# Two neighbouring weight slots filled by one transfer, in a fused block of two attention mixers

## The chip, the cores and the metric

The kernel runs on one core of one Trainium2 chip. The metric is the device time of one launch in microseconds; the median of three runs stands for a kernel. One more execution is profiled, and its trace gives the rows below. Engines are named as the profile names them: PE is TensorE (PEld its weight loads), DVE VectorE, ACT ScalarE, POOL GpSimd, SP SyncE, which here only issues transfers.

## What is computed

One layer on 256 tokens of width 2048, in float32: a normalisation, one input projection to 9296 columns, two groups of eight attention heads, gating, an output projection, the residual and a last normalisation.

```python
h = rms_norm(x, norm_gain[l])
proj = jnp.einsum('btd,de->bte', h, w_in[l])
qa, ka, va, ga, qb, kb, vb, gb, qi, ki, wi = jnp.split(proj, offsets, axis=-1)
out_a = chunked_relpos_attention(heads(qa, H_A), heads(ka, H_A), heads(va, H_A), rel_bias[l])
out_b = dsa_sparse_attention(heads(qb, H_B), heads(kb, H_B), heads(vb, H_B), qi, ki, wi, slopes)
ya = out_a.reshape(B, T, D_A) * jax.nn.silu(ga)
yb = out_b.reshape(B, T, D_B) * jax.nn.silu(gb)
x = x + jnp.einsum('bte,ed->btd', jnp.concatenate([ya, yb], axis=-1), w_out[l])
return rms_norm(x, final_gain)
```

Mixer A is softmax attention with a learned bias by relative position; with 256 tokens its band covers all earlier chunks of 64. Mixer B picks the 64 best keys of each query by an indexer (`qi`, `ki`, `wi`) and attends to these with a distance penalty.

## The kernel before

**Blocks and units.** The weights of both projections are read once, as 22 blocks of 512 columns (numbers 0 to 21). Blocks 0 and 1 make values (1 with the narrow index columns beside), 2 and 3 the indexer's queries, 4 to 7 queries and keys of mixer B, 8 and 9 the remaining values, 10 to 13 queries and keys of mixer A, 14 to 17 the gates, 18 to 21 the output projection. A block has 8 units; a unit is 256 rows by 512 columns of weights, 512 KB, laid out as 128 partitions of 4 KB.

**The ring.** A unit passes through a ring of RING = 4 slots. SyncE loads it into `w_raw[:, u % 4]` and counts on `w_landed[u % 4]`. ScalarE's `split_hi` (L752 to L759) rounds it to float32r into `hi_slots`; it waits for the landing and for `mm_done`, TensorE's count of finished units, because TensorE must have read the slot four units back. VectorE's `split_lo` (L1076 to L1081) subtracts and writes what is left to `lo_slots`, and counts `lo_done`. TensorE's `unit` (L520 to L529) waits for `lo_done` and runs 12 matmuls of 512 columns: two row blocks, two token tiles, three products (hi by hi, hi by lo, lo by hi). Since `split_lo` is the last reader of the raw slot, SyncE may load a unit as soon as `lo_done` counts the unit four back.

**The order on the engines** is written out by hand. Each engine runs its own list in order and waits on semaphores. In the pair blocks (10 to 17) each block g carries, between the splits, the attention of one head pair, pair = g - 10. On ScalarE (`pair_attention`, L973): exponentials, split of unit 6, `planes_out` (L951: the probabilities' 32-bit words are taken apart into two planes of 16 bits), split of unit 7, the splits of units 0 and 1 of the next block, staging of the next pair's queries and keys, `pT_out` (L956: wait for the turned planes, put the words together again, L958, round, L960), split of unit 2, `projection_out` of the block just finished, splits of units 3 to 5. VectorE has the same splits in its list, with `pT_rest` (L1429) after those of units 0 and 1. TensorE runs `score_pair` after unit 1 of block g and `value_pair` (L692), which waits for `pT_rest`, after unit 0 of block g + 1. There is one value_pair per pair; that of pair 7 stands after unit 2 of block 18.

**Turns.** Activations that are needed with tokens and features exchanged are turned by transposing transfers on 16-bit planes. SyncE issues them, in between the loads, from the same queue: `turn_planes(pair)` (L385) after the load of unit 2 of block g + 1, and `turn_projection(n)` (L410) after the load of unit 6. n = 0 to 3 are queries and keys of mixer B, 4 to 7 those of mixer A, 8 to 11 the gates; the planes of n are made by VectorE (n < 4) or GpSimd, and put together by ScalarE or GpSimd. The last of them, n = 11, is issued in block 18; its product, the last gates, goes through ScalarE's `tanh_gates` and VectorE's `gated`, then `y_hi` and `y_lo` (L1469, with `ylo_done`), and TensorE waits for `y_lo(6)` before unit 6 of block 18. A turn waits for its planes first (`planes_made`, `proj_split`), and while it waits, the loads behind it wait as well.

**The loads that the change touches** are those of blocks 4 to 17 (`token_block`, L401) and 18 to 21 (`out_unit`, L426, the last three blocks in a hardware loop): 144 loads, each behind a wait on `lo_done`.

Of the kernel before, what the change touches and what calls it, by code (L numbers as in the profile page):

```python
# [43 lines left out]
G_TOKENS = 4  # L44
G_WIDE, G_QI, G_INDEX, G_VB, G_VA, G_QKA, G_GATE, G_OUT, G_END = 1, 2, 3, 8, 9, 10, 14, 18, 22
ROW_VB, VA_FIRST, ROW_VA = 6, 8, 9
UK = 2
UNITS = KT // UK
RING = 4
# [9 lines left out]
def hybrid_block(nc, xT, x, norm_gain, w_blocks, w_narrow, rel_bias, wo_blocks, final_gain, out):  # L59
# [6 lines left out]
    ds = bass.ds  # L66

    with ExitStack() as ctx:
        def sb(name, shape, dt=f32):
            return ctx.enter_context(nc.sbuf_tensor(name, shape, dt))  # L70
# [4 lines left out]
        def sem(name):  # L75
            return ctx.enter_context(nc.semaphore(name))
# [5 lines left out]
        w_raw = raw_slots[:, :, 0:UK * CB]  # L82
# [13 lines left out]
        o = sb("o", [P, 4, TM, CB])  # L96
# [56 lines left out]
        w_landed = [sem(f"w_landed{s}") for s in range(RING)]  # L153
        hi_done = sem("hi_done")
        lo_done = sem("lo_done")
# [130 lines left out]
        rows = (slice(0, IDX_D), slice(IDX_D, P))  # L286
# [35 lines left out]
        def narrow_loads(p):  # L322

            return sum(kind == BROAD and q % RING == p % RING for q, (kind, _) in enumerate(STARTS[:p + 1]))
# [15 lines left out]
        def _(sp):  # L340
            def load(u, src):
                sp.dma_start(w_raw[:, u % RING, :], src).then_inc(w_landed[u % RING], 16)


            def load_features(u, rows):
                half, j = u // 4, u % 4
                c = (j % 2) * CB + half * T
                sp.dma_start(w_raw[:, u % RING, :].rearrange("p (q c) -> p q c", q=4),
                             rows[:, 4 * (j // 2):4 * (j // 2) + 4, c:c + T]).then_inc(w_landed[u % RING], 16)
# [10 lines left out]
            for u in range(HALVED):  # L360
                for kk in range(UK):
                    c = slice(kk * CB, kk * CB + CB)
# [22 lines left out]
            def turn_planes(pair):  # L385
                sp.wait_ge(planes_made, pair + 1)
                sp.dma_start_transpose(flat(planes_T).rearrange("p (t q) -> p t q", q=P),
                                       flat(planes)).then_inc(planes_turned, 16)
# [10 lines left out]
                        turn_small(*turns)  # L399

            def token_block(g, row, pair=None, n=None):  # L401
                for u in range(UNITS):
                    sp.wait_ge(lo_done, g * UNITS + (u - RING + 1))
                    load(u, w_blocks[ds(row, 1), u, :, :].rearrange("o p c -> (o p) c"))
                    if u == 2 and pair is not None:
                        turn_planes(pair)
                    if u == 6 and n is not None:
                        turn_projection(n)

            def turn_projection(n):  # L410
                sp.wait_ge(proj_split, n + 1)
                source, turned = proj_planes(n)
                sp.dma_start_transpose(flat(turned).rearrange("p (t q) -> p t q", q=P),
                                       flat(source)).then_inc(proj_turned, 16)
# [3 lines left out]
            for g in range(G_TOKENS, G_VA):  # L418
                token_block(g, g - G_QI if g < G_VB else ROW_VB + 1, n=g - G_TOKENS - 1 if g > G_TOKENS else None)
            token_block(G_VA, ROW_VA)  # L420
            token_block(G_QKA, G_QKA)
            for pair in range(HEADS - 1):
                g = pair + G_QKA + 1
                token_block(g, g, pair, pair + N_LATE)

            def out_unit(g, u):  # L426
                sp.wait_ge(lo_done, g * UNITS + (u - RING + 1))
                load(u, wo_blocks[ds(g - G_OUT, 1), u, :, :].rearrange("o p c -> (o p) c"))

            for u in range(UNITS):  # L430
                out_unit(G_OUT, u)
                if u == 2:
                    turn_planes(HEADS - 1)
                if u == 6:
                    turn_projection(N_END - 1)
            with sp.Fori(G_OUT + 1, G_END) as g:
                for u in range(UNITS):
                    out_unit(g, u)

            for n, (m, c) in enumerate(VECTOR_PARTS):  # L440
                sp.wait_ge(vector_scaled, n + 1)
# [309 lines left out]
        def _(act):  # L751
            def split_hi(g, c):  # L752

                u = c % UNITS
                s = u % RING
                act.wait_ge(w_landed[s], g * (16 * UNITS // RING) + 16 * (c // RING + 1))
                if not (isinstance(g, int) and g * UNITS + c < RING):
                    act.wait_ge(mm_done, g * UNITS + (c - RING + 1))
                nc.scalar.activation(hi_slots[:, s, 0:UK * CB], w_raw[:, s, :], ACT.Copy).then_inc(hi_done, 1)  # L759
# [55 lines left out]
            for p, (kind, u) in enumerate(STARTS):  # L815
                if p >= 2 * HALVED:
                    if kind == PLAIN:
                        act.wait_ge(xT_landed[u], 16)
                        for k in range(UK * u, UK * u + UK):
                            a_part(k)  # L820
                        split_hi(0, p)
                    else:
                        split_hi_wide(p)
                    for v in SQUARES.get(p, ()):
                        square_x(v)
                if p == len(STARTS) - 2:
                    nc.scalar.preload_act_table(ACT.Sqrt)
# [7 lines left out]
            for c in range(4):  # L835
                split_hi(G_QI, c)
# [4 lines left out]
            for c in range(4, 8):  # L841
                split_hi(G_QI, c)
                if c == 6:
                    features_low(G_QI, 0, QT)
# [165 lines left out]
            g = G_OUT - 1  # L1010
# [570 lines left out]
```

## Time and profile before

| | us |
|---|---|
| median of three runs | 516.11 (516.06 to 516.22) |
| the profiled execution | 516.02 |
| its span, first to last instruction | 514.2 |
| TensorE busy | 505.7 |
| VectorE busy | 354.3 |
| ScalarE busy | 305.7 |
| GpSimd busy | 70.1 |
| weight transfers (mean of all 16 transfer engines, over the span) | 67.4% of their time |

The difference between the profiled execution's time and its span lies ahead of the first and behind the last instruction of the program. Busy time is an average over the whole span; what a wait costs is read from the stretch in which it happens. A matmul's end is modelled, so successive matmuls overlap in the trace: what counts is the distance of their starts.

### The profile page before, as it was taken

To read this page: it belongs to the slowest core of one execution; us is meant where nothing else is said; L and a number is where in the kernel's file an instruction comes from. 1 tells how busy PE (TensorE), PEld (TensorE's weight loads), DVE (VectorE), ACT (ScalarE), POOL (GpSimd) and SP (SyncE) were. 2 spreads that over 40 slices of the span, in tenths; PEclk is the share of its full clock that TensorE was granted. 3 is DMA by queue.
4 is the path that set the end of the run, shared out by engine and by line. 5 is a ranking of instruction groups with operands and counts; after the bars stand their busy time and mean duration, and the time that the engine had idled before them with its cause. 6 is when DMAs were issued, how large, how long until landed. Compare 5 with 4: busy or idle time off the path is not lost.

```text
span 514.2 us, 6764 instructions
## 1 busy us (share of the span) xinstructions
PE 505.7 (98%) x2476; PEld 430.1 (84%) x2476; DVE 354.3 (69%) x517; ACT 305.7 (59%) x410; POOL 70.1 (14%) x61
## 2 busy tenths in 40 slices
PE   8999999999999999999999999999999999999994
PEld 6989999888888888888888888888888888888883
DVE  5897777765856686876777766666768687746554
ACT  6866555446564555445866758584959586545342
POOL 1000053150500000000111130303021313000000
PEclk9999999999999999999999999999999999999998
DMA  8974898658685876563768676877677779775614
GB/s 270 401 234 142 215 296 265 241 184 237 236 256 164 246 208 224 201 193 102 246 198 240 212 245 215 214 216 205 194 206 229 233 222 267 266 223 178 202 41 164
DMA packets 77358, 112.23 MB, mean 218 GB/s; under 512 B 44144, under 2 KB 53264, under 8 KB 77200
## 3 DMA queue, kind: packets, MB, share of 16 engines
q1 hardware_dynamic: 75472, 106.38, 67.4%
q0 software_dynamic: 1568, 5.01, 3.0%
q10 hardware_dynamic: 288, 0.46, 0.3%
q8 instruction: 17, 0.28, 0.2%
q14 instruction: 13, 0.11, 0.1%
HBM read 99.24 MB, written 2.11 MB: 197 GB/s over the span
## 4 chain that ended last, share of the span: by engine, by line
PE 98%; DMA 1%; DVE 0%; ACT 0%; issue 0%; DVEq 0%; POOLq 0%
PE acc L516 26%; PE acc L518 25%; PE acc L517 25%; PE acc L547 5%; PE acc L567 4%; PE acc L575 3%; PE acc L551 2%; PE aux L577 2%; DMA gain<-norm_gain 1%; PE aux L688 1%; PE aux L698 1%; PE aux L686 0%; PE aux L703 0%; PE aux L704 0%; PE aux L685 0%; PE aux L705 0%
## 5 line engine op out<-in xcount | busy, mean ns | idle before, releaser
L1080 DVE TENSOR_TENSOR lo_slots<-raw_slots,hi_slots 128x1024 fp32r<-128x1024 f32 x166 | 210.4, 1278 | 108.7 <-ACT hi_slots L759 108.1
L759 ACT ACTIVATE hi_slots<-raw_slots 128x1024 fp32r<-128x1024 f32 x166 | 174.0, 1056 | 127.4 <-PE acc L518 110.0
L516 PE MATMUL acc<-hi_slots,acts 128*128 128x512 f32 x576 | 225.4, 391 | 0.0
L518 PE MATMUL acc<-hi_slots,acts 128*128 128x512 f32 x576 | 224.2, 389 | 0.0
L517 PE MATMUL acc<-lo_slots,acts 128*128 128x512 f32 x576 | 224.2, 389 | 0.0
L518 PEld LDWEIGHTS acc<-hi_slots,acts 128*128 128x128 f32 x576 | 108.1, 188 | 22.8
L516 PEld LDWEIGHTS acc<-hi_slots,acts 128*128 128x128 f32 x576 | 108.2, 188 | 22.1 <-DVE acts L1471 0.3
L517 PEld LDWEIGHTS acc<-lo_slots,acts 128*128 128x128 f32 x576 | 108.2, 188 | 21.8
L547 PE MATMUL acc<-acts,hi_slots 128*128 128x384 f32 x128 | 34.3, 349 | 0.0
L491 POOL COPY o<-z 128x2048 uint16<-128x2048 uint16 x4 | 7.6, 1899 | 159.7 <-ACT z L874 159.7
L551 PEld LDWEIGHTS acc<-acts,lo_slots 128*128 128x128 f32 x128 | 23.1, 188 | 0.0
L551 PE MATMUL acc<-acts,lo_slots 128*128 128x192 f32 x128 | 23.1, 262 | 0.0
L547 PEld LDWEIGHTS acc<-acts,hi_slots 128*128 128x128 f32 x128 | 19.4, 191 | 0.0
L944 ACT ACTIVATE probs<-probs,neg_top,q_rate 128x256 f32<-128x256 f32 (+1 forms) x16 | 8.6, 536 | 17.4 <-DVE neg_top L1392 17.4
L567 PE MATMUL acc<-hi_slots,acts 128*128 128x512 f32 x64 | 17.9, 394 | 0.3 <-DVE acts L1109 0.3
L575 PE MATMUL acc<-hi_slots,acts 128*128 128x320 f32 x64 | 18.0, 308 | 0.0
L577 PE MATMUL aux<-hi_slots,acts 128*128 128x272 f32 x64 | 17.6, 286 | 0.0
L958 ACT ACTIVATE probs_T<-qiT 128x1536 uint16<-128x1536 uint16 x8 | 15.6, 1947 | 2.3 <-DMA qiT<-qiT 2.3
L491 POOL COPY v<-z 128x2048 uint16<-128x2048 uint16 x4 | 8.0, 2010 | 53.7 <-ACT z L874 53.7
L497 POOL COPY z<-t_gate 128x2048 uint16<-128x2048 uint16 x4 | 12.1, 3024 | 21.4 <-DMA t_gate<-v 21.4
L567 PEld LDWEIGHTS acc<-hi_slots,acts 128*128 128x128 f32 x64 | 11.5, 188 | 3.9 <-DVE acts L1109 1.7
L947 ACT ACTIVATE probs<-probs,neg_max 128x256 f32<-128x256 f32 (+1 forms) x16 | 7.1, 446 | 11.8 <-DVE neg_max L1388 11.8
(172 smaller groups left out, 481.5 us busy)
## 6 DMA issues: line engine op xcount, KB each, us to landing
raw_slots<-w_blocks SPq DMA_DIRECT2D x140, 512.0 KB, 4.3
raw_slots<-wo_blocks SPq DMA_DIRECT2D x32, 512.0 KB, 4.2
raw_slots<-w_blocks SPq DMA_DIRECT2D x8, 256.0 KB, 5.2
qk<-xT SPq DMA_DIRECT2D x7, 256.0 KB, 5.3
qk<-x POOLq DMA_DIRECT2D x1, 1536.0 KB, 8.1
o<-ext_dram POOLq DMA_DIRECT2D x1, 1024.0 KB, 7.3
fgain<-final_gain POOLq DMA_DIRECT2D x1, 1024.0 KB, 4.8
out<-o SPq DMA_DIRECT2D x2, 512.0 KB, 3.0
```

Source lines behind the costliest of these rows:

```text
L491: nc.gpsimd.tensor_copy(proj_planes(n)[0], halves(z)).then_inc(proj_split, 1)
L516: nc.tensor.matmul(dst, a_hi[:, k, t], hi, start=start, stop=False)
L517: nc.tensor.matmul(dst, a_hi[:, k, t], lo, start=False, stop=False)
L518: return nc.tensor.matmul(dst, a_lo[:, k, t], hi, start=False, stop=stop)
L547: nc.tensor.matmul(whole, w_hi4[:, u % RING, q, f * HD:f * HD + HD], acts[:, k, :, tokens], start=(k == 0), stop=False)
L551: last = nc.tensor.matmul(acc[:, bank:bank + n], w_lo4[:, u % RING, q, f * HD:f * HD + HD], a_hi[:, k, tokens], start=False, stop=(k == KT ...
L567: last = nc.tensor.matmul(acc[:, m * CB:m * CB + CB], a[:, k, m * P:m * P + P], w[:, p % RING, c], start=start, stop=stop)
L575: nc.tensor.matmul(acc[:, (TM + m) * CB:(TM + m) * CB + PART], a[:, k, t], w[:, p % RING, c:c + PART], start=start, stop=stop)
L577: last = nc.tensor.matmul(aux[m][:, 0:REST], a[:, k, t], w[:, p % RING, c + PART:c + WIDE], start=start, stop=stop)
L759: nc.scalar.activation(hi_slots[:, s, 0:UK * CB], w_raw[:, s, :], ACT.Copy).then_inc(hi_done, 1)
L958: nc.scalar.activation(halves(probs_T), planes_T, ACT.Copy).then_inc(words_made, 1)
L1080: nc.vector.tensor_tensor(lo_slots[:, s, 0:UK * CB], w_raw[:, s, :], hi_slots[:, s, 0:UK * CB].bitcast(f32), ALU.subtract).then_inc(lo_don ...
```

## The change

From block 4 on, SyncE loads two units with one transfer of 1 MB into slots 0 and 1 or slots 2 and 3. The transfer waits for what its second unit's load waited for, and counts on the semaphore of the first slot alone; ScalarE waits on that semaphore for both units. So 144 transfers become 72. The turns keep their place behind the transfer that has unit 2, or unit 6; that transfer has unit 3, or unit 7, in it now. Nothing changes on VectorE, TensorE and GpSimd.

```diff
             def load(u, src):
                 sp.dma_start(w_raw[:, u % RING, :], src).then_inc(w_landed[u % RING], 16)
 
+            def load_two(g, u, rows):
+                sp.wait_ge(lo_done, g * UNITS + (u + 1 - RING + 1))
+                sp.dma_start(w_raw[:, u % RING:u % RING + 2, :],
+                             rows[:, u:u + 2, :, :].rearrange("o u p c -> p (o u) c")).then_inc(w_landed[u % RING], 16)
+
...
             def token_block(g, row, pair=None, n=None):
-                for u in range(UNITS):
-                    sp.wait_ge(lo_done, g * UNITS + (u - RING + 1))
-                    load(u, w_blocks[ds(row, 1), u, :, :].rearrange("o p c -> (o p) c"))
+                for u in range(0, UNITS, 2):
+                    load_two(g, u, w_blocks[ds(row, 1), :, :, :])
                     if u == 2 and pair is not None:
                         turn_planes(pair)
                     if u == 6 and n is not None:
...
-            def out_unit(g, u):
-                sp.wait_ge(lo_done, g * UNITS + (u - RING + 1))
-                load(u, wo_blocks[ds(g - G_OUT, 1), u, :, :].rearrange("o p c -> (o p) c"))
-
-            for u in range(UNITS):
-                out_unit(G_OUT, u)
+            def out_units(g, u):
+                load_two(g, u, wo_blocks[ds(g - G_OUT, 1), :, :, :])
+
+            for u in range(0, UNITS, 2):
+                out_units(G_OUT, u)
                 if u == 2:
                     turn_planes(HEADS - 1)
                 if u == 6:
                     turn_projection(N_END - 1)
             with sp.Fori(G_OUT + 1, G_END) as g:
-                for u in range(UNITS):
-                    out_unit(g, u)
+                for u in range(0, UNITS, 2):
+                    out_units(g, u)
...
                 s = u % RING
-                act.wait_ge(w_landed[s], g * (16 * UNITS // RING) + 16 * (c // RING + 1))
+                together = not isinstance(g, int) or g * UNITS + c >= G_TOKENS * UNITS
+                act.wait_ge(w_landed[s - s % 2 if together else s], g * (16 * UNITS // RING) + 16 * (c // RING + 1))
```

## Rows read from the trace of the kernel before

**Rows 1.** The page: busy time, and the chain that ended last

```profile
PE 505.7 (98%) x2476; PEld 430.1 (84%) x2476; DVE 354.3 (69%) x517; ACT 305.7 (59%) x410; POOL 70.1 (14%) x61
PE 98%; DMA 1%; DVE 0%; ACT 0%; issue 0%; DVEq 0%; POOLq 0%
```

**Rows 2.** By stretch: us; PE, PEld, DVE, ACT, POOL busy; PEclk; DMA; GB/s

```profile
79.00:507.00 428.00, 428.00 (x2007) 358.96 (x2005) 290.87 (x416) 253.63 (x338) 60.09 (x37) 1.00 0.69 211
507.00:514.00 7.00, 0.02 (x1) 0.00 (x0) 2.76 (x6) 1.84 (x4) 0.00 (x0) 0.76 0.54 202
```

**Rows 3.** Groups by line: busy, mean ns, idle before and its releasers

```profile
L759 ACT ACTIVATE hi_slots<-raw_slots 128x1024 fp32r<-128x1024 f32 x166 | 174.0, 1056 | 127.4 <-PE acc L518 110.0 <-PE acc L551 7.1 <-DMA raw_slots<-w_blocks 4.0
```

**Rows 4.** Timeline of SyncE's queue, pair 0: start us, duration, instruction

```profile
243.01 0.33 SPq L342 DMA_DIRECT2D raw_slots<-w_blocks  x1
243.39 1.54 SPq L387 DMA_TRANSPOSE qiT<-qiT  x1
245.60 0.48 SPq L342 DMA_DIRECT2D raw_slots<-w_blocks  x1
```

**Rows 5.** Timeline of SyncE's queue: pair 4's turn, the last projection turn

```profile
337.36 2.27 SPq L387 DMA_TRANSPOSE qiT<-qiT  x1
422.40 2.60 SPq L413 DMA_TRANSPOSE t_gate<-v  x1
```

**Rows 6.** Timeline, pairs 0, 1, 3, 4, 7: copy, low part, value_pair

```profile
251.00 0.69 DVE L1432 TENSOR_TENSOR parts_lo<-probs_T,parts_hi 128x512 fp32r<-128x512 f32 x1 [2.22 <-ACT parts_hi L960]
252.07 0.38 PE L698 MATMUL aux<-probs_T,v 128*128 128x128 f32 x2
274.43 0.69 DVE L1432 TENSOR_TENSOR parts_lo<-probs_T,parts_hi 128x512 fp32r<-128x512 f32 x1 [1.82 <-ACT parts_hi L960]
276.22 0.38 PE L698 MATMUL aux<-probs_T,v 128*128 128x128 f32 x2
321.89 0.69 DVE L1432 TENSOR_TENSOR parts_lo<-probs_T,parts_hi 128x512 fp32r<-128x512 f32 x1 [1.89 <-ACT parts_hi L960]
324.53 0.38 PE L698 MATMUL aux<-probs_T,v 128*128 128x128 f32 x2
342.88 1.94 ACT L958 ACTIVATE probs_T<-qiT 128x1536 uint16<-128x1536 uint16 x1
345.51 0.69 DVE L1432 TENSOR_TENSOR parts_lo<-probs_T,parts_hi 128x512 fp32r<-128x512 f32 x1 [1.48 <-ACT parts_hi L960]
348.68 0.49 PE L698 MATMUL aux<-probs_T,v 128*128 128x128 f32 x3
419.83 1.97 ACT L958 ACTIVATE probs_T<-qiT 128x1536 uint16<-128x1536 uint16 x1
```

**Rows 7.** Timeline of the first output block: VectorE and TensorE

```profile
423.45 1.23 DVE L1080 TENSOR_TENSOR lo_slots<-raw_slots,hi_slots 128x1024 fp32r<-128x1024 f32 x1 [0.26 <-ACT hi_slots L759]
435.27 0.68 DVE L1471 TENSOR_TENSOR acts<-o,acts 128x512 fp32r<-128x512 f32 x1
435.47 0.39 PE L517 MATMUL acc<-lo_slots,acts 128*128 128x512 f32 x1
435.70 0.39 PE L518 MATMUL acc<-hi_slots,acts 128*128 128x512 f32 x1
436.01 0.50 PE L516 MATMUL acc<-hi_slots,acts 128*128 128x512 f32 x1
```

**Rows 8.** Stretches as rows 2; landing of L387's, L413's turns; loads issued

```profile
149.00:151.50 2.50, 2.50 (x13) 2.07 (x12) 0.17 (x1) 2.30 (x3) 0.00 (x0) 1.00 1.02 419
243.90:245.90 2.00, 2.00 (x10) 1.68 (x9) 1.55 (x2) 2.00 (x3) 0.00 (x0) 1.00 0.79 239
DMA to landing us min/median/max: 4.8/4.9/5.0
DMA to landing us min/median/max: 4.3/4.4/6.6
raw_slots<-w_blocks SPq DMA_DIRECT2D x140, 512.0 KB, 4.3
```

## Prediction

> **What bounds the kernel now.** I read the page's engine line and chain of waits first [rows 1]: TensorE is busy for 98% of the span, and the chain that ended last is TensorE for 98%. Then the busy time by stretches [rows 2]: from 79 to 507 us, the whole stretch that the change touches, TensorE is busy for 428 of 428 us; only the last 7 us are not matmul. Two things follow. No part of the weight stream is on the path today: no load can make the time shorter by landing earlier, since no matmul waits for one. And any wait that is new for TensorE is paid in full, because there is no idle time of TensorE later that could take it back. So the question is only whether something that TensorE needs becomes later than TensorE. The waits say how the stream runs [rows 3]: ScalarE's high-part splits wait 110 us for TensorE to give their slot back, and for a load of w_blocks only twice, 4.0 us. The loads have room. I then looked, row by row, at what else SyncE issues: the transposing transfers ("turns").
>
> **Fewer, larger loads.** 144 loads of 512 KB become 72 of 1 MB. The even unit of each pair now leaves with the odd one, one unit later (a unit is 12 matmuls that start 0.23 us apart [rows 7], 2.7 us), and lands with the whole megabyte. Price of the second half in the transfer engines: in a stretch with loads queued one behind the other they move 419 GB/s, so 1.25 us [rows 8]; while a lone load starts up, 239 GB/s, so 2.2 us. The even unit is thus 4 to 5 us later at its slot. I price that at nothing: ScalarE waits for TensorE and not for the load [rows 3], and behind its split stand the other slots of the ring, split and not yet multiplied. That ring of four is the cover; if it were gone, each late load would cost its lateness in full. SyncE's saved issues (0.33 us each [rows 4]) are off the path: worth 0.
>
> **The turn of the probabilities, eight times.** For each head pair SyncE issues the turn (L387) after the load of unit 2. In pair 0 the load leaves at 243.01, the turn 0.38 later at 243.39, as soon as ScalarE has made the planes, and the load of unit 3 at 245.60 [rows 4]. The load of unit 3 is the interesting row: it goes as soon as the low-part split of unit 7 of the block before is done. In the changed kernel units 2 and 3 are one transfer that waits for just that split, and the turn stands behind it. So the turn leaves at 245.60 + 0.38 = 245.98, 2.6 us later. The same distance of some 2.2 us stands between turn and next load in the other pairs, since the split of unit 7 follows the planes on ScalarE, and its low part that on VectorE, in a fixed order.
> On top comes the queue. A turn takes 4.8 to 5.0 us from issue to landing with 512 KB issued 0.38 us ahead of it; the projection turns, whose load went out 1.8 us earlier, take as little as 4.3 [rows 8]. So a turn waits behind the load in front of it, and a load of twice the size should cost it the second half: between 0 and 2.2 us. I take 1.25, the rate of queued loads, because the second half follows on a stream that is already running. Delay of the landing: 2.6 + 1.25 = 3.85 us (2.6 to 4.8).
>
> Who waits for it: ScalarE copies the turned planes (L958, L960), VectorE splits off the low part (L1432), then TensorE's value_pair (L698) starts, after unit 0 of the next block. Queued behind the copy on ScalarE are the high-part splits of the next units; they have more room than value_pair. How much room: the end of L1432 against the start of L698 [rows 6]. Pair 0: 251.69 and 252.07, 0.38 us. Pair 1: 275.12 and 276.22, 1.1. Pair 3: 322.58 and 324.53, 1.95; pair 2 lies between, near 1.7. Pair 4: 346.20 and 348.68, 2.48, and there ScalarE was busy with its list until 342.88 while the turn landed at most 5.0 after its issue at 337.36 [rows 5, 8], so 0.5 more: 3.0. Pairs 5 and 6 repeat pair 4. In pair 7 ScalarE reaches its copy at 419.83, 4.5 us later than three further blocks of 24.15 (324.53 to 348.68) would put it: no cost. When TensorE does wait it loses a little more: at 436.01 it starts 0.06 after VectorE's row ends and that matmul takes 0.50 instead of 0.39 [rows 7], so I take 0.17 off each room.
> Since the score of the next pair is a TensorE step behind value_pair, each wait moves the next pair's chain along with TensorE; the next pair has its old room and pays again. Pair 0: 3.85 - 0.2 = 3.65. Pair 1: 2.9. Pair 2: 2.3. Pair 3: 2.05. Pairs 4 to 6: 3.85 - 2.8 = 1.05 each, 3.1. Sum 14.0 us.
>
> **The turn of the gate projection, at the end.** The projection turns (L413) stand behind unit 6's load and will stand behind units 6 and 7. Of twelve, the first four also wait for VectorE's plane copy, which comes after the split that gates the new load, and what the next seven bring is read a block or more later: 0, the cover being that block. The last one has no block behind it. It leaves at 422.40 [rows 5], and GpSimd joins the words, which VectorE's and ScalarE's gating wait for, down to the low part of the gated activations (L1471, ends 435.95), on which TensorE's row at 436.01 already waits [rows 7]. The new transfer of units 6 and 7 waits for the low-part split that begins at 423.45 and ends at 424.68 [rows 7]; the turn leaves 0.4 later, at 425.07: 2.67 us late. It also falls from 1.8 us behind 512 KB to 0.38 behind 1 MB. Bounds for that: 0, and the second half plus the lost distance, 2.2 + 1.4. I take 2.2: the megabyte lands 1.25 after the 4.3 us that a half takes [rows 8], 5.2 after the turn's own issue, and the turn some 1.5 us after that, 6.7 where it now takes about 4.5. Sum 4.9 us.
>
> **Sum.** The profiled execution took 516.02 us (span 514.2, the rest around it), 0.1 below the median of the three runs. 516.0 + 14.0 + 4.9 = 534.9; on the median's scale **535.0 us**. With the queue's price at 0: 2.4 + 1.7 + 1.1 + 0.8 + 2.7 = 8.7, 524.8. With the half at 239 GB/s: eight more places with 0.95 each, 542.5.
>
> **Rivals.**
> *The queue costs the turns nothing.* Only the 2.6 us of later issue remain: 524.8 as above. For it: the turn's transfer might be prepared while the load still runs. Against: a turn right behind a load already takes 0.6 longer than one with distance [rows 8]. It is also where we would land if VectorE and ScalarE won back, during TensorE's first wait, what later pairs lack. Chance 0.14.
> *The queue costs more*, the half at start-up rate: 542.5. For it: the load in front of a turn is always the first after a pause. Chance 0.1.
> *TensorE's clock falls during the waits.* The granted clock is 1.00 (2.4 GHz) through the whole busy stretch and 0.76 on average over the last 7 us, where TensorE has nothing to do: there it fell to the lower level [rows 2]. The two longest waits, 3.65 at pair 0 and 4.9 at the end, are the candidates. At 1.2 GHz the 0.23 us of a matmul double, so one unit at the low level costs 2.7 us more: two such, 540.3. The Trainium skill says so too ("TensorE: Matmul & The Clock Gate", Part 1): the throttled state is the default and activity releases it, so idling has a price after the idling. The trace agrees as far as its last row goes; no wait inside the busy stretch shows it. Chance 0.2.
> *Not slower.* With half as many transfers to issue and complete, the turn passes the queue faster than now and lands when it is needed. It decides at 0.2 us of delay in pair 0 and 0 at the end. To get there a turn would have to win 2.4 us of 4.9, and the best projection turn, with its load well ahead, took 4.3 [rows 8]. A gain beyond that isn't there to be had, as TensorE has no wait to lose. Time 516.0. Chance 0.05, of which 0.01 is a run that comes out faster.
> *A load becomes late*, in the stretches where ScalarE already reaches its split as the load lands: more than 543. By my estimate a megabyte would have to take twice what I price. Chance 0.04.
>
> **How the numbers follow.** The forecast as summed has 0.47. The range takes the queue's two bounds, 524.7 to 542.5; the clock's case lies in it. What is left out is the not slower case, the late load and part of the tails. A measurement here tells about 0.2% (1 us) from no change; all cases but one are far over it: slower 0.95, same 0.04, faster 0.01.
>
> **What would show it.** In the trace of after: waits of TensorE at L698 for VectorE L1432, largest in the first pair and shrinking to about 1 us in pairs 4 to 6, none in pair 7; one wait of about 5 us before unit 6 of block 18 for L1471; turns that leave 0.4 behind their load and land 6 us or more after issue; ScalarE's L958 waiting for the turn in pairs 0 to 6. If TensorE waits at L516 for L1080 instead, it is the loads. If the turns land 5 us after issue, the queue's price was wrong; if the waits at L698 don't come back pair after pair, the assumption that the chain moves along with TensorE was. If L698 doesn't wait at all, the step on the room is wrong.

## The result: 559.9 us, and the profile after

The changed kernel takes 559.86 us (median of four runs, 557.09 to 564.97) against 516.16 us before: 1.086 times as long (95% interval 1.082 to 1.090). Forecast were 535.0 us and a range of 524.7 to 542.5. The direction came as predicted, and so did the way in which the late turns of the probabilities stop TensorE; most of what is missing comes from two terms that the sum has at nothing. The profiled execution of after took 561.64 us, 1.8 above the median; its span is 559.8 us, 45.6 more than before, and the readings below are made against that span.

The page of after: busy time, the chain that ended last, and three groups by line (busy, mean ns, idle before and releaser).

```profile
PE 520.7 (93%) x2476; PEld 440.1 (79%) x2476; DVE 362.3 (65%) x517; ACT 305.3 (55%) x410; POOL 66.7 (12%) x61
PE 23%; DMA 11%; ACT 9%; DVE 9%; issue 4%; SPq 1%; POOL 0%; DVEq 0%; ACTq 0%; POOLq 0%
L701 PE MATMUL aux<-probs_T,v 128*128 128x128 f32 x32 | 7.1, 356 | 23.6 <-DVE parts_lo L1436 23.6
L519 PE MATMUL acc<-hi_slots,acts 128*128 128x512 f32 x576 | 229.4, 398 | 7.0 <-DVE acts L1475 7.0
L962 ACT ACTIVATE probs_T<-qiT 128x1536 uint16<-128x1536 uint16 x8 | 15.4, 1921 | 32.7 <-DMA qiT<-qiT 32.7
```

The lines have moved by 3 to 5 (value_pair L698 is L701, `split_lo` L1080 is L1084, the copy L958 is L962, the low part L1432 is L1436, the turns L387 and L413 are L392 and L417, GpSimd's join L497 is L500). In place of 98% TensorE [rows 1], the chain now runs through the turns (DMA), their copies on ScalarE and the low parts on VectorE. TensorE waits 23.6 us at value_pair, in seven pairs, and 7.0 us once, before unit 6 of block 18. And it is busy for 15.0 us more with the same 2476 matmuls. This says why, by stretches (columns as in [rows 2]): seven stretches of the busy part in which the granted clock is 0.50, the lower of the two levels (1.2 GHz).

```profile
255.02:261.85 6.83, 4.26 (x15) 3.88 (x16) 4.07 (x4) 5.56 (x7) 1.89 (x1) 0.50 0.16 67
316.46:319.87 3.41, 3.41 (x11) 2.74 (x11) 2.54 (x3) 2.13 (x3) 1.89 (x1) 0.50 0.00 0
343.77:350.60 6.83, 5.88 (x19) 5.11 (x20) 5.17 (x4) 4.16 (x6) 1.89 (x1) 0.50 0.09 10
374.49:377.90 3.41, 3.41 (x14) 3.12 (x15) 2.47 (x2) 3.08 (x5) 1.89 (x1) 0.50 0.02 5
405.21:408.62 3.41, 3.41 (x10) 2.62 (x9) 2.54 (x3) 1.79 (x2) 1.89 (x1) 0.50 0.00 0
432.51:435.92 3.41, 3.41 (x13) 2.97 (x12) 2.54 (x2) 2.68 (x4) 1.89 (x1) 0.50 0.00 0
476.89:483.72 6.83, 3.96 (x9) 3.14 (x10) 6.72 (x8) 5.17 (x6) 0.00 (x0) 0.50 0.74 271
sum 34.13, PE 27.74 PEld 23.58 DVE 26.05 ACT 24.57 POOL 11.36; mean PE 3.96 PEld 3.37 DVE 3.72 ACT 3.51 POOL 1.62
```

Two matmuls of 512 columns in the second of these stretches, from TensorE's timeline:

```profile
317.20 0.63 PE L520 MATMUL acc<-lo_slots,acts 128*128 128x512 f32 x1
317.63 0.63 PE L521 MATMUL acc<-hi_slots,acts 128*128 128x512 f32 x1
```

TensorE worked for 27.74 us in the seven stretches. Such matmuls start 0.427 us apart there, elsewhere 0.227, so by this spacing 27.74 x (1 - 0.227/0.427) = 13.0 us of the time is the clock. The whole difference then reads: 24.8 us of waits at value_pair (from the end of the matmul before, by starts), 7.2 at the end, 0.4 early (at 128.6 us, where ScalarE's copy waits 1.9 us for the first projection turn, which landed 7.6 us after its issue in place of 4.6), 13.0 of clock. Sum 45.4 of 45.6.

The timeline of pair 0 and of the end, SyncE's queue, ScalarE, VectorE and TensorE:

```profile
245.84 0.37 SPq L346 DMA_DIRECT2D raw_slots<-w_blocks  x1
246.25 1.97 SPq L392 DMA_TRANSPOSE qiT<-qiT  x1
254.24 1.91 ACT L962 ACTIVATE probs_T<-qiT 128x1536 uint16<-128x1536 uint16 x1 [6.65 <-DMA qiT<-qiT]
256.84 0.69 DVE L1436 TENSOR_TENSOR parts_lo<-probs_T,parts_hi 128x512 fp32r<-128x512 f32 x1 [7.82 <-ACT parts_hi L964]
257.59 1.22 PE L701 MATMUL aux<-probs_T,v 128*128 128x128 f32 x4 [5.13 <-DVE parts_lo L1436]
...
457.18 1.06 ACT L763 ACTIVATE hi_slots<-raw_slots 128x1024 fp32r<-128x1024 f32 x1 [3.17 <-DMA raw_slots<-wo_blocks]
464.14 0.37 SPq L346 DMA_DIRECT2D raw_slots<-wo_blocks  x1
464.55 5.14 SPq L417 DMA_TRANSPOSE t_gate<-v  x1
471.82 2.46 POOL L500 COPY z<-t_gate 128x2048 uint16<-128x2048 uint16 x1 [10.47 <-DMA t_gate<-v]
479.76 0.80 PE L519 MATMUL acc<-hi_slots,acts 128*128 128x512 f32 x1 [7.01 <-DVE acts L1475]
```

Here the predicted chain is to be seen link by link: the load, the turn 0.41 behind it at 246.25 (before 243.39 [rows 4]; ScalarE's planes are only 0.2 us later than in the kernel before), ScalarE waiting for the landing, VectorE, TensorE. What was not predicted is how late it lands: 7.96 us after its issue.

Landing of the turns in after, the planes' (L392) and the projections' (L417); before it was 4.9 and 4.4 in the median [rows 8]:

```profile
DMA to landing us min/median/max: 6.4/6.6/8.7
DMA to landing us min/median/max: 5.6/7.1/9.2
```

### The profile page after: what moved, and what is told of

Its sections match the earlier page's. It is cut to its first block, busy times and chain, and to the rows that moved or that the text cites. A ratio compares the mean times of both kernels' runs of the same rounds, so it can differ in the third digit from the quotient of the medians.

```text
span 559.8 us, 6656 instructions
## 1 busy us (share of the span) xinstructions
PE 520.7 (93%) x2476; PEld 440.1 (79%) x2476; DVE 362.3 (65%) x517; ACT 305.3 (55%) x410; POOL 66.7 (12%) x61
## 4 chain that ended last, share of the span: by engine, by line
PE 23%; DMA 11%; ACT 9%; DVE 9%; issue 4%; SPq 1%; POOL 0%; DVEq 0%; ACTq 0%; POOLq 0%
DMA qiT<-qiT 8%; PE acc L519 7%; PE acc L520 7%; PE acc L521 7%; DVE lo_slots L1084 3%; ACT hi_slots L763 3%; ACT probs_T L962 3%; DVE probs L1430 2%; DMA raw_slots<-wo_blocks 1%; DMA t_gate<-v 1%; ACT probs L948 1%; PE aux L701 1%; ACT probs L951 1%; DVE parts_lo L1436 1%; DVE probs L1407 1%
## 5 line engine op out<-in xcount | busy, mean ns | idle before, releaser
L1084 DVE TENSOR_TENSOR lo_slots<-raw_slots,hi_slots 128x1024 fp32r<-128x1024 f32 x166 | 211.4, 1285 | 111.9 <-ACT hi_slots L763 111.3
L519 PE MATMUL acc<-hi_slots,acts 128*128 128x512 f32 x576 | 229.4, 398 | 7.0 <-DVE acts L1475 7.0
L520 PE MATMUL acc<-lo_slots,acts 128*128 128x512 f32 x576 | 227.9, 396 | 0.0
L521 PE MATMUL acc<-hi_slots,acts 128*128 128x512 f32 x576 | 227.3, 395 | 0.0
L519 PEld LDWEIGHTS acc<-hi_slots,acts 128*128 128x128 f32 x576 | 110.9, 193 | 30.1 <-DVE acts L1475 7.4
L521 PEld LDWEIGHTS acc<-hi_slots,acts 128*128 128x128 f32 x576 | 110.4, 192 | 23.6
L520 PEld LDWEIGHTS acc<-lo_slots,acts 128*128 128x128 f32 x576 | 110.5, 192 | 22.4
L962 ACT ACTIVATE probs_T<-qiT 128x1536 uint16<-128x1536 uint16 x8 | 15.4, 1921 | 32.7 <-DMA qiT<-qiT 32.7
L1436 DVE TENSOR_TENSOR parts_lo<-probs_T,parts_hi 128x512 fp32r<-128x512 f32 x8 | 5.5, 692 | 41.5 <-ACT parts_hi L964 41.5
L701 PE MATMUL aux<-probs_T,v 128*128 128x128 f32 x32 | 7.1, 356 | 23.6 <-DVE parts_lo L1436 23.6
L701 PEld LDWEIGHTS aux<-probs_T,v 128*128 128x128 f32 x32 | 5.4, 235 | 26.7 <-DVE parts_lo L1436 26.6
L550 PEld LDWEIGHTS acc<-acts,hi_slots 128*128 128x128 f32 x128 | 19.4, 191 | 0.0
L570 PE MATMUL acc<-hi_slots,acts 128*128 128x512 f32 x64 | 18.1, 397 | 0.0
L958 ACT ACTIVATE qiT<-probs 128x1536 uint16<-128x1536 uint16 x8 | 11.9, 1485 | 11.3 <-DVE probs L1430 11.3
```

What stands on the lines that cost most here:

```text
L519: nc.tensor.matmul(dst, a_hi[:, k, t], hi, start=start, stop=False)
L520: nc.tensor.matmul(dst, a_hi[:, k, t], lo, start=False, stop=False)
L521: return nc.tensor.matmul(dst, a_lo[:, k, t], hi, start=False, stop=stop)
L550: nc.tensor.matmul(whole, w_hi4[:, u % RING, q, f * HD:f * HD + HD], acts[:, k, :, tokens], start=(k == 0), stop=False)
L570: last = nc.tensor.matmul(acc[:, m * CB:m * CB + CB], a[:, k, m * P:m * P + P], w[:, p % RING, c], start=start, stop=stop)
L701: nc.tensor.matmul(aux[3][:, h * T + P:h * T + T], v1_flat[:, c], pT1[:, h, :], start=(h == 0), stop=False, skip_group_check=True)
```

## The experiments

The main theory: the turns stand one unit later and behind a whole megabyte, and what hangs on them stops TensorE; the clock falls on top. Rivals: the larger transfer itself is slow or starves the ring; the planes' turns alone do it; or the clock is the larger half and the waits the smaller.

### Each turn ahead of the transfer

After, with each turn issued before the load that it stood behind (in the first output block alike):

```diff
                 for u in range(0, UNITS, 2):
-                    load_two(g, u, w_blocks[ds(row, 1), :, :, :])
                     if u == 2 and pair is not None:
                         turn_planes(pair)
                     if u == 6 and n is not None:
                         turn_projection(n)
+                    load_two(g, u, w_blocks[ds(row, 1), :, :, :])
...
```

> The 72 transfers of 1 MB stay, but each turn is issued ahead of the transfer of units 2 and 3 (or 6 and 7) and not behind it. If the late turns are the whole loss (A), TensorE has no wait for VectorE's L1432 or L1471 split rows again and the time is that of before, 516 us, within 2 us. If the megabyte loads come too late for the splits (B; ScalarE's idle time for loads grew from 6.4 to 23.5 us in the changed kernel), the waits for loads stay and the time stays over 530 us.

Measured: 523.80 us, 1.014 of before (1.0125 to 1.0159), between the two expected cases. So 36 of the 44 us are the turns' place behind the loads, with all that follows from it. No wait at value_pair is left, and the planes' turns land in 3.7 us, faster than in the kernel before; the landing of L392 and of the projection turns (L417), and three waits (total, times, longest):

```profile
DMA to landing us min/median/max: 3.6/3.7/3.7
DMA to landing us min/median/max: 4.3/4.3/4.9
...
ACT hi_slots L763 <- DMA raw_slots<-w_blocks: 52.7, 26, 6.8
PE aux L627 <- ACT t_gate L864: 3.6, 2, 1.9
PE acc L519 <- DVE lo_slots L1084: 1.5, 1, 1.5
```

The 3.7 us is what the prediction lacked: the price of a planes' turn with nothing in front of it. The 7.6 us that stay are paid elsewhere. ScalarE waits 52.7 us for loads (4.0 before [rows 3]), since a turn that waits for its planes now holds up the load of two units; in blocks 5 and 6 the split that ScalarE is late with stands ahead of a copy (L864) that TensorE's L627 needs, 1.9 us at most, with 3.4 us at the lower clock behind the second wait; and once, in block 19, a low part is late, behind a load that landed 9.9 us after its issue while GpSimd's 1.5 MB transfer of x ran.

### The old transfers, the turns one unit later

Before, with the planes' turns behind unit 3's load and the projections' behind unit 7's; the loads stay 512 KB:

```diff
-                    if u == 2 and pair is not None:
+                    if u == 3 and pair is not None:
                         turn_planes(pair)
-                    if u == 6 and n is not None:
+                    if u == 7 and n is not None:
                         turn_projection(n)
...
```

> The kernel before, with its 144 loads of 512 KB, and only the turns moved: the turn of the probabilities behind the load of unit 3, the projection's behind that of unit 7. The turn leaves 2.6 us later as in the changed kernel, but with two loads of 512 KB ahead of it, one of them 2.6 us older. (A) order and transfer size share the loss: turns land about 5 us after issue instead of 6.5, waits of about 2.4, 1.7, 1.1 and 0.8 us in pairs 0 to 3, 3 us at the end: 525 to 530 us. (B) the loads alone: 516 us. (C) the order alone is the loss, the queue costs nothing: as the changed kernel, 555 to 562 us.

Measured: 540.10 us, 1.045 (1.0427 to 1.0480), more than expected. The wait at value_pair (total, times, longest), the landing of the turns (L387), and VectorE and GpSimd in pair 4:

```profile
PE aux L698 <- DVE parts_lo L1432: 14.1, 7, 3.5
...
DMA to landing us min/median/max: 4.8/4.9/7.1
...
347.80 3.26 DVE L1426 TENSOR_SCALAR probs<-probs,p_inv 128x256 f32<-128x256 f32 x4
...
348.01 2.52 POOL L497 COPY qk<-o 128x2048 uint16<-128x2048 uint16 x1 [7.35 <-DMA o<-o]
```

The later issue was as expected, 2.6 us in every pair, and the turns landed after 4.8 to 4.9 us in pairs 1 to 6 (6.4 in pair 0). But by starts the waits at value_pair were 3.69, 2.65, 1.65, 1.63, 1.88, 1.85 and 1.90, where they should have fallen to next to nothing by pair 4 by the rooms of [rows 6]; 3.1 us stood at the end, and 10.2 us passed at the lower clock. In pairs 3 to 6 the four normalising rows of VectorE (L1426), 1.01 us in all in the kernel before, took 2.1 to 3.3 us: GpSimd's join of a projection turn had moved onto them. In pairs 1 and 2 it stood on a row ahead of them (L1392, 2.52 and 2.09 us in place of 0.23). That was the first sight of a term that the prediction has at nothing.

### Old transfers in pairs

Before, with two 512 KB loads issued back to back where the megabyte would go, the turns behind both:

```diff
-                for u in range(UNITS):
-                    sp.wait_ge(lo_done, g * UNITS + (u - RING + 1))
-                    load(u, w_blocks[ds(row, 1), u, :, :].rearrange("o p c -> (o p) c"))
+                for u in range(0, UNITS, 2):
+                    sp.wait_ge(lo_done, g * UNITS + (u + 1 - RING + 1))
+                    for v in (u, u + 1):
+                        load(v, w_blocks[ds(row, 1), v, :, :].rearrange("o p c -> (o p) c"))
...
```

> The changed kernel's order and gates, but each 1 MB transfer issued as two of 512 KB, one right after the other on the same queue, 144 transfers again. (A) what delays a turn is the bytes that stand ahead of it: turns land 6.4 us after issue as behind the single megabyte, and the time is 556 to 562 us, half a microsecond a pair more for the second issue. (B) if a transfer of 1 MB is slow by its size, two halves let the turn pass sooner: about 5 us to landing, and 540 us as with the order alone.

Measured: 558.38 us, 1.081 (1.0773 to 1.0846), the time of the changed kernel with none of its 1 MB transfers, and as expected. The queue in pair 2 and the landing of the planes' turns (L387):

```profile
305.54 0.80 SPq L342 DMA_DIRECT2D raw_slots<-w_blocks  x2
306.39 2.21 SPq L387 DMA_TRANSPOSE qiT<-qiT  x1
...
DMA to landing us min/median/max: 5.9/6.0/8.1
```

What the turn pays is the megabyte in front of it, whether that is one transfer or two. The kernel with the order alone lost 24 us; the even unit's bytes, moved into the turn's way, lose the other 18 to 20. The size of a transfer is worth nothing either way.

### Large transfers only where turns go first

Before, with 1 MB transfers in blocks 10 to 17 alone and the turns ahead of them there; blocks 4 to 9 and 18 to 21 as before:

```diff
+                for u in range(0, UNITS, 2):
+                    if g < G_QKA:
+                        for v in (u, u + 1):
...
+                        continue
                     if u == 2 and pair is not None:
...
+                    load_two(g, u, w_blocks[ds(row, 1), :, :, :])
...
```

> Turns first as in the run of that name, and the 1 MB transfers in blocks 10 to 17 alone; blocks 4 to 9 and 18 to 21 load 512 KB in the order of the kernel before. (A) the 7.3 us that were left with all turns first are three waits, two in blocks 5 and 6 (a pair of loads stuck behind a turn that waits for its planes) and one in block 19 (a pair behind GpSimd's 1.5 MB transfer); without pairs there they go: 516 to 517 us. (B) if the larger transfers cost TensorE something in every block, the pair blocks keep it: 520 us or more.

Measured: 516.17 us, 1.0001 (0.9992 to 1.0011), as expected. Its page, and the stretch of [rows 2]:

```profile
PE 505.8 (98%) x2476; PEld 430.4 (84%) x2476; DVE 354.4 (69%) x517; ACT 306.2 (60%) x410; POOL 70.6 (14%) x61
PE 98%; DVE 0%; ACT 0%; DVEq 0%; issue 0%
79.00:507.00 428.00, 427.87 (x2005) 358.81 (x2003) 291.01 (x417) 254.27 (x338) 60.53 (x37) 1.00 0.67 211
```

Eight of the eighteen blocks from block 4 on come in 1 MB transfers here, and nothing is lost or won: TensorE is busy throughout, as in the kernel before. So what the kernel with all turns first still lost belongs to blocks 4 to 9 and 18 to 21, and large transfers have no gain to give, because no load is on the path.

### Planes first, projections first

Two halves of the first experiment. The planes' turns alone ahead of their transfer:

```diff
                 for u in range(0, UNITS, 2):
-                    load_two(g, u, w_blocks[ds(row, 1), :, :, :])
                     if u == 2 and pair is not None:
                         turn_planes(pair)
+                    load_two(g, u, w_blocks[ds(row, 1), :, :, :])
                     if u == 6 and n is not None:
...
```

> The changed kernel with the turns of the probabilities ahead of the transfer of units 2 and 3; the projection turns stay behind units 6 and 7. (A) no wait at value_pair is left, since the turns land 3.7 us after issue as in the run with all turns first; the joins of GpSimd still come late, but no chain is short any more; the wait of 7 us before unit 6 of block 18 and the low clock behind it stay, and the 0.4 us of the early blocks: 516 + 7 + 2 + 1 = 526 us. (B) If late joins cost by themselves, through VectorE's splits, there are waits in blocks 12 to 16 as well: over 530 us.

The projection turns alone:

```diff
                 for u in range(0, UNITS, 2):
+                    if u == 6 and n is not None:
+                        turn_projection(n)
                     load_two(g, u, w_blocks[ds(row, 1), :, :, :])
                     if u == 2 and pair is not None:
                         turn_planes(pair)
-                    if u == 6 and n is not None:
-                        turn_projection(n)
...
```

> The changed kernel with the projection turns ahead of the transfer of units 6 and 7; the turns of the probabilities stay behind units 2 and 3. (A) the end's wait of 7 us goes, with the low clock behind it (about 2 us), and GpSimd's joins come 1.5 to 4 us earlier and off VectorE's normalising rows, which took 3.35 us instead of 1.01 in pair 5: 1 to 2 us less in pairs 2 to 5. Together 559.9 - 7 - 2 - 6 = about 545 us. If GpSimd does not matter, about 551 us. If the end was the loads' doing, 558 us or more.

Measured: 526.29 us with the planes first (1.020; 1.0180 to 1.0214), as expected, and 551.61 with the projections first (1.069; 1.0622 to 1.0751). The second is more than expected, and by the time alone it is the case in which GpSimd does not matter; its rows say otherwise. With the planes first no pair waits for long (the longest 0.06 us), although the normalising rows took 3.2 to 3.3 us in three pairs; the end waits as in after, and the clock is low in and behind that wait. The wait (total, times, longest), and that stretch:

```profile
PE acc L519 <- DVE acts L1475: 7.1, 1, 7.1
...
439.46:449.70 10.24, 5.33 (x13) 4.17 (x14) 7.88 (x10) 7.21 (x9) 0.45 (x1) 0.50 0.74 258
```

With the projections first the end is all but free of that wait (0.3 us), and the joins end before the normalising. The wait at value_pair, and pair 4's rows of VectorE and GpSimd in the timeline:

```profile
PE aux L701 <- DVE parts_lo L1436: 18.4, 7, 5.1
...
384.89 1.01 DVE L1430 TENSOR_SCALAR probs<-probs,p_inv 128x256 f32<-128x256 f32 x4
...
382.16 2.52 POOL L500 COPY z<-t_gate 128x2048 uint16<-128x2048 uint16 x1 [4.41 <-DMA t_gate<-v]
```

In pairs 0 to 5 the four rows take 1.01 us there (2.19 in pair 6), and the waits at value_pair add to 19.6 us in place of 24.8, behind the same late turns (6.4 to 6.7 us, 7.95 in pair 0). By their own durations the rows account for 7.4 us less; other steps of the chain give 2 back, most of it in pair 3, where the join now stands on an earlier row (L1396, 1.67 us in place of 0.23) and the wait stays (3.56, in after 3.50). So the GpSimd term is one of its own, and it goes with the projection turns. The full time did not fall as far as that, because the waits that the first experiment had in blocks 5 and 6 came in here too (2.0 and 1.7 us), another of 2.4 us for a late low part stood at the end, and 17.1 us still passed at the lower clock (6.3 us by the spacing). With these the sum comes to 546.7 of a span of 548.3.

### Keeping TensorE at work in the waits

To price the clock apart from the waits, after with matmuls put into the waits whose product is not read: ten short ones ahead of each value_pair and 30 ahead of unit 6 of block 18 (first), or four to eight long float32 ones (second).

```diff
...
             def value_pair(pair):
+                if pair < HEADS - 1:
+                    filler(KT - 1, 10)
                 pe.wait_ge(pt_lo_done, pair + 1)
...
             for u in range(UNITS):
+                if u == 6:
+                    filler(0, 30)
                 pe.wait_ge(ylo_done, u + 1)
...
```

> The changed kernel with matmuls that nobody reads in TensorE's list: 10 of 512 columns ahead of each value_pair of pairs 0 to 6 (2.3 us), 30 ahead of unit 6 of block 18 (6.8 us), so that TensorE works in most of the time that it spent waiting. (A) the clock: the changed kernel's TensorE is busy for 15 us more with the same matmuls, because the granted clock goes to its lower level after the waits; with work in the waits it stays at the upper one and the time falls by 8 to 13 us, to 547 to 552 us, though 100 matmuls (22.7 us) were added. If the clock is not the cause, the added work costs time or nothing: 560 us or more.

```diff
...
             def value_pair(pair):
+                if pair < HEADS - 1:
+                    filler(KT - 1, 4 if pair else 6)
                 pe.wait_ge(pt_lo_done, pair + 1)
...
             for u in range(UNITS):
+                if u == 6:
+                    filler(0, 8)
                 pe.wait_ge(ylo_done, u + 1)
...
```

> The changed kernel with few but long matmuls that nobody reads in TensorE's waits: plain float32 of 512 columns (about 0.85 us each), 6 ahead of value_pair 0, 4 ahead of value_pairs 1 to 6, 8 ahead of unit 6 of block 18; 38 in all, 32 us. The run with 100 short ones grew its turns to 8 us, as a 16 KB instruction transfer fell into each of them, so it left the clock open. (A) the clock stays at its upper level, the matmuls lose their 13 us, the fillers exceed the waits by some 2 us: 547 to 551 us. (B) if the clock's cost was misread: 560 us or more with turns still at 6.5 us.

Measured: 567.05 us (1.094; 1.0876 to 1.1002) and 560.30 us (1.084; 1.0819 to 1.0868). Both miss what was expected. The short ones left 2.6 to 3.1 us of the waits of pairs 0 to 5 idle, and the clock still fell, 20.5 us in six stretches. The long ones did hold it: 3.4 us low in all, against 34.1. Yet the time did not fall, for a reason outside the question. In the second kernel, the stretch around pair 0's wait (columns as in [rows 2], the clock at 1.00), the landing of the turns (L392), what the transfer engines' queues carried while pair 1's turn ran, and the wait that was left there:

```profile
256.00:262.00 6.00, 5.92 (x27) 3.92 (x26) 3.60 (x3) 5.20 (x7) 1.89 (x1) 1.00 0.13 55
...
DMA to landing us min/median/max: 6.9/8.0/8.5
...
q8 instruction: 1, 0.02, 0.7%
...
288.49 0.71 PE L708 MATMUL aux<-probs_T,v 128*128 128x128 f32 x4 [2.44 <-DVE parts_lo L1445]
```

The turns of pairs 0 to 5 took 7.8 to 8.3 us where after has 6.4 to 6.6: in both programs a 16 KB transfer of instructions fell into every planes' turn, as it does in after in pair 0 alone. So the experiment changed two things at once, and no run shows the price of the clock by itself. The traces together do. Take off each span all of TensorE's waits, by starts and with the fillers counted as waiting; what is then left above the 514.2 us of the kernel before goes with the time at the lower clock:

| kernel | at the lower clock, us | left over, us | by the spacing, us |
|---|---|---|---|
| old transfers in pairs | 30.7 | 13.7 | 13.1 |
| after | 34.1 | 13.3 | 13.0 |
| projections first | 17.1 | 7.9 | 6.3 |
| the order alone | 10.2 | 5.1 | 4.7 |
| long fillers | 3.4 | 2.4 | 1.6 |
| large transfers in blocks 10 to 17 | 0 | 0.0 | 0 |

The last column is TensorE's work in those stretches, priced as above. It stays within 1.7 us of what is left over, in the three kernels that are not listed too. Where the long fillers held the clock up, only 2.4 us are left over after 42 us of waits and fillers; after has 13.3 behind 32 us of waits. So the 13 us in after are the clock's.

## Why the prediction was wrong, and where it was right

**Right.** TensorE had no wait to spare and the loads did not starve in the pair blocks; the turn goes out 2.6 us later in pairs 0 to 5 (2.6 forecast; 3.7 in pair 6); it does wait behind the second half of the megabyte; the wait comes back pair after pair because the chain moves along with TensorE (from the first matmul of score TensorE takes 20.0 us until it could start value_pair, in each of the pairs 0 to 6, before and after); pair 7 costs nothing, though its room fell from 3.4 to 0.6 us; one wait for the last projection turn stands before unit 6 of block 18.

**Wrong: two terms at nothing, and two sizes.** The step that failed first is "what the next seven bring is read a block or more later: 0": the projection turns do cost, through GpSimd's copies beside VectorE's rows, 8.6 us. The second is the lower clock, kept out of the sum as a rival: 13.0 us. Besides, the queue and the end were sized too low. The sum by its terms, those of value_pair over pairs 0 to 6; the room is what the kernel before had between the end of L1432 and the moment TensorE needed it, and its measured value is the remainder of the other rows:

| term, us | forecast | measured |
|---|---|---|
| turns issued later | 18.2 | 19.4 |
| turns slower, issue to landing | 8.8 | 12.9 |
| normalising rows (four of L1430 in each pair) longer | 0 | 8.6 |
| room, and what the chain wins back | -12.9 | -16.1 |
| waits at value_pair | 14.0 | 24.8 |
| wait for the last projection turn | 4.9 | 7.2 |
| early wait, at 128.6 us | 0 | 0.4 |
| lower clock | 0 | 13.0 |

*The queue's price, 1.25 us taken within 0 to 2.2.* It is 1.5 to 1.8 in pairs 1 to 6, within those bounds, and 3.0 in pair 0. The price was the rate of queued loads, 419 GB/s; the second half cost more than that rate gives. The comparison in [rows 8] that was to support it was misread: it took a projection turn with distance to its load (4.3) as a turn without a queue and the planes' turn (4.9) as one with, and found 0.6 for half a megabyte. A projection turn carries 128 x 2048 elements and a planes' turn 128 x 1536; alone the one takes 4.25 and the other 3.7, as the turns-first kernel shows. So 512 KB in front cost a planes' turn 1.2 us all along, and a megabyte costs it 2.8, as it does a projection turn (7.0 to 7.2 us in after, without an instruction transfer). In pair 0 an instruction transfer of 16 KB came on top, 1.4 us.

*The projection turns at n = 4 to 10, priced at nothing.* Their readers had the block that was named as cover. But the turn lands later, and GpSimd's join (L500) with it, and the join is itself a load on VectorE. Pair 5 of after, VectorE and GpSimd:

```profile
386.31 3.35 DVE L1430 TENSOR_SCALAR probs<-probs,p_inv 128x256 f32<-128x256 f32 x4
...
386.34 2.52 POOL L500 COPY z<-t_gate 128x2048 uint16<-128x2048 uint16 x1 [8.64 <-DMA t_gate<-v]
```

Four rows that take 1.01 us start with the copy and end after it; one of them alone takes 2.70 us. The Trainium skill states the mechanism ("SBUF — State Buffer", section "SBUF: two separate sides"): VectorE, in some of its modes or with two SBUF inputs, and GpSimd share a pair of ports under an exclusive lock that the loser waits out for the whole instruction. The trace agrees: 3.35 us is about the copy's 2.52 and the rows' own 1.01. In which mode the rows run no trace shows. The same was to be seen in the kernel before, where a small row of VectorE (0.23 us elsewhere) stands beside a join, while the reduction just ahead of it (L1388), beside the same join, keeps its 0.68 us:

```profile
260.48 1.37 DVE L1392 TENSOR_SCALAR neg_top<-neg_max,q_rate 128x2 f32<-128x2 f32 x1
...
259.33 2.50 POOL L497 COPY qk<-o 128x2048 uint16<-128x2048 uint16 x1 [4.40 <-DMA o<-o]
```

*The end, 4.9 forecast, 7.2 measured.* The turn did go 2.7 us later for its place and landed 2.7 us slower (7.15 after issue, forecast 6.7). But the transfer ahead of it waits for a split that ScalarE reached 2.9 us later still, behind the wait for a load at 457.18 (the timeline above). That is the one place where the step "loads land later: nothing" failed: GpSimd issues a 512 KB load of x at 448.75, when it has joined the turn before (itself slow, 8.45 us), and the weights' megabyte issued 0.8 us later took 7.65 us, where its neighbours took 5.2 to 6.0. (With the planes first the two also overlap, 7.1 us; no run keeps them apart, so this cause is argued.) GpSimd's last join was 1.1 us shorter than before, so 5.6 + 2.7 - 1.1 = 7.2.

*The clock.* It was a rival with a chance of 0.2, two places and 5.4 us. The mechanism was right and the number of places was not: it fell at six of the seven pairs that waited and at the end, 34.1 us in all, 13.0 of cost. It named only the two longest waits as candidates, and waits of 2.4 to 3.6 us at value_pair were enough. Once eight waits stood in the sum it belonged into the forecast: at its own price of 2.7 us a place, eight places are 21.6 us, where seven were measured to cost 13.0.

The rival that large transfers would help themselves fell: with them in blocks 10 to 17 the time is that of before to 0.1%. The Trainium skill ("DMA: Bandwidth & Descriptors", section "Measured (HBM→SBUF, 128 partitions, SWDGE, issued from GpSimd)") advises batches of 1 MiB and more for bandwidth, as measured on transfers that GpSimd issues; here SyncE issues them. The landing agrees as far as it goes (5.4 us for 1024 KB in after, 4.3 for 512 KB [rows 8]), but the rate of a transfer that nobody waits for has no price, and the time of one that waits behind it does.

Open are what makes the weights' load before the end slow, and what decides into which turn an instruction transfer falls.

## What to carry to other kernels

A larger transfer is not only fewer issues: everything small that shares its queue waits for the later gate and for the added bytes, so read what stands behind each load in the queue before merging loads, and move the latency-bound transfer ahead of it. Price a queue from two transfers of the same size, one with and one without the load in front. Where TensorE is busy throughout, a sum of several new waits is to be raised by the lower clock after them, and a transfer that lands later also moves the copies on other engines that it triggers: look what stands beside their new time.

## What the runs showed of the hardware

**Instruction transfers.** The page lists a queue of the kind "instruction", 17 transfers of 16 KB in after, roughly one in each 30 us. One that falls into a planes' turn makes it about 1.4 us slower: 7.96 us in pair 0 against 6.4 to 6.6 in the others of after, 6.4 against 4.8 in the kernel with the order alone, 7.4 against 6.0 in that with old transfers in pairs. Pair 6 of the long fillers is an exception, 6.9 with one.

**The clock after short waits.** In the kernel before, the lower level did not occur in the busy stretch. In after it came in or right after six of seven waits of 2.4 to 5.3 us at value_pair. The length of a wait alone does not decide: in the turns-first kernel a wait of 1.85 us was followed by 3.41 us at the lower level, one of 2.0 us was not, and in after pair 1's, 3.06 us, was not either.
